# Layer norms of a two-block transformer kernel: gamma and beta applied on token rows by VectorE, layers unrolled

## The reference, cut to what matters

```python
def _layernorm(x, g, b):
    mu = jnp.mean(xf, -1, keepdims=True)
    xc = xf - mu
    var = jnp.mean(xc * xc, -1, keepdims=True)
    y = xc * lax.rsqrt(var + LN_EPS) * g + b

for l in range(DEPTH_2):          # 2 layers
    x = _layernorm(ALPHA * x + 0.5 * _swiglu(x, ffn1_w_in[l], ffn1_w_out[l]), ln1_g[l], ln1_b[l])
    mix = _hybrid_mixer(x, l, ...)        # attention, state space and stick-breaking branches
    x = _layernorm(ALPHA * x + mix, ln2_g[l], ln2_b[l])
    x = _layernorm(ALPHA * x + 0.5 * _swiglu(x, ffn2_w_in[l], ffn2_w_out[l]), ln3_g[l], ln3_b[l])
```

## Time and profile before

| what | us |
|---|---|
| median of three runs | 2288.71 |
| span of the profiled execution | 2284.1 |
| TensorE matmul busy | 2143.6 (94%) |
| VectorE busy | 1436.7 (63%) |
| ScalarE busy | 1127.0 (49%) |
| GpSimd busy | 140.9 (6%) |
| granted TensorE clock, mean | 0.966 |

### The profile page before, as it was taken

How to read it: one execution, slowest core, us unless ns; L and a number is a source line. 1 busy time by engine, 2 the same in 40 slices (tenths; PEclk the granted TensorE clock), 3 DMA queues, 4 the chain that set the end, 5 groups by cost and what they waited for, 6 DMA issues and landing times.

```text
span 2284.1 us, 38164 instructions
## 1 busy us (share of the span) xinstructions
PE 2143.6 (94%) x14507; PEld 1938.2 (85%) x14507; DVE 1436.7 (63%) x2106; ACT 1127.0 (49%) x1783; POOL 140.9 (6%) x157
## 2 busy tenths in 40 slices
PE   6999899999979999999979979997999999997997
PEld 5788799799868899888979959986989988897995
DVE  6766688465566676566665555556667656666555
ACT  4576466344335586355434433344458635543432
POOL 1200000000010003100010010001000310001002
PEclk9999999999989999999989989998999999998998
DMA  6433455544635344333535544563534333353562
GB/s 220 158 119 125 145 184 184 185 151 163 225 135 190 120 143 132 129 111 112 178 118 184 203 148 148 173 219 129 184 124 136 130 130 111 111 185 112 184 206 88
DMA packets 271155, 350.25 MB, mean 153 GB/s; under 512 B 9915, under 2 KB 225693, under 8 KB 271005
## 3 DMA queue, kind: packets, MB, share of 16 engines
q1 hardware_dynamic: 270733, 347.19, 45.3%
q0 software_dynamic: 272, 1.05, 0.1%
HBM read 347.17 MB, written 1.05 MB: 152 GB/s over the span
## 4 chain that ended last, share of the span: by engine, by line
issue 84%; PE 9%; POOL 4%; DVE 2%; ACT 0%; DMA 0%; SPq 0%; POOLq 0%; DVEq 0%; ACTq 0%
PE ps L650 3%; PE ps L652 2%; PE ps L651 2%; POOL act_s L2186 2%; POOL x L2174 1%; POOL x L2176 1%; DVE ring_r L1531 0%; DMA ring<-in_w_in 0%; PE ps L792 0%; PE ps L820 0%; PE ps L805 0%; POOL small L2151 0%; PE ps L757 0%; DVE act_s L1805 0%; DVE xT_r L1531 0%
## 5 line engine op out<-in xcount | busy, mean ns | idle before, releaser
L1531 DVE TENSOR_TENSOR ring_r<-ring,ring_hi 128x1024 fp32r<-128x1024 f32 x642 | 780.3, 1224 | 539.9 <-ACT ring_hi L1108 536.9
L1108 ACT ACTIVATE ring_hi<-ring 128x1024 fp32r<-128x1024 f32 x642 | 674.9, 1058 | 792.4 <-PE ps L652 737.8
L650 PE MATMUL ps<-xT_hi,ring_hi 128*128 128x256 f32 x2912 | 835.2, 287 | 36.9 <-DVE xT_r L1531 20.3
L651 PE MATMUL ps<-xT_r,ring_hi 128*128 128x256 f32 x2912 | 823.2, 283 | 0.0
L652 PE MATMUL ps<-xT_hi,ring_r 128*128 128x256 f32 x2912 | 823.0, 283 | 0.0
L650 PEld LDWEIGHTS ps<-xT_hi,ring_hi 128*128 128x128 f32 x2912 | 555.6, 191 | 52.3 <-issue 29.9
L651 PEld LDWEIGHTS ps<-xT_r,ring_hi 128*128 128x128 f32 x2912 | 555.6, 191 | 0.1
L652 PEld LDWEIGHTS ps<-xT_hi,ring_r 128*128 128x128 f32 x2912 | 555.1, 191 | 0.0
L652 PE MATMUL ps<-ring_hi,tok_r 128*128 128x512 f32 x536 | 212.6, 397 | 0.0
L650 PE MATMUL ps<-ring_hi,xT_hi 128*128 128x512 f32 x432 | 178.5, 413 | 15.3 <-DVE xT_r L1531 11.5
L651 PE MATMUL ps<-ring_r,xT_hi 128*128 128x512 f32 x432 | 174.2, 403 | 0.0
(11 more groups left out here) (280 smaller groups left out, 2616.7 us busy)
## 6 DMA issues: line engine op xcount, KB each, us to landing
ring<-in_w_mix_in SPq DMA_DIRECT2D x92, 1024.0 KB, 4.9
ring<-in_ffn_w_in SPq DMA_DIRECT2D x88, 1024.0 KB, 5.0
ring<-in_ffn_w_out SPq DMA_DIRECT2D x44, 1024.0 KB, 4.9
ring<-in_w_branch SPq DMA_DIRECT2D x24, 1024.0 KB, 5.3
ring<-in_w_in SPq DMA_DIRECT2D x22, 1024.0 KB, 5.0
ring<-in_w_ffn_up SPq DMA_DIRECT2D x22, 1024.0 KB, 5.0
ring<-in_w_ffn_down SPq DMA_DIRECT2D x11, 1024.0 KB, 5.0
ring<-in_w_mix_out SPq DMA_DIRECT2D x8, 1024.0 KB, 5.0
```

What stands on the lines that cost most here:

```text
L650: pe.matmul(out_, stat[0], mov[0], start=first, stop=False)
L651: pe.matmul(out_, stat[0], mov[1], start=False, stop=False)
L1108: act.activation(half_of(ring_hi[:, s % HIGHS, :], s, q), half_of(ring[:, s % SLOTS, :], s, q), ACT.Copy).then_inc(w_hi, 1)
L1531: return dve.tensor_tensor(lo, whole, hi.bitcast(F32), ALU.subtract)
```

## The change

It is one rewrite of all norms, with what follows from it.

- VectorE applies gamma and beta on token rows, in place in `x`: x minus mean times gamma, then times inverse root plus beta, four `scalar_tensor_tensor` of 128x512 a tile. ScalarE's `xhat` and GpSimd's `residual` are gone; GpSimd keeps the roots.
- TensorE transposes `x` itself, each group of four blocks as soon as its half row is normed (`rows_normed`). ScalarE copies all four groups from PSUM into `xT_hi`, and VectorE subtracts them from the same PSUM banks into `xT_r`. The plain `xT` is no longer written.
- The order on VectorE around a norm is by token tile, and each piece of 128x512 is added as soon as its own products are done. The last slot of an FFN's down product is ordered so that each of the four pieces ends by itself.
- `ahead` is 1 for all FFNs, so one slot of the next run is split ahead of every norm; `after_norm` is gone.
- RMS gains arrive as broadcast rows (three more DMAs of 512 KB, those of `ln` gamma and beta as rows are gone) and are multiplied in on VectorE, two pieces of 128x512 a tile; the norm of `mem` is made in place.
- The loop over layers is unrolled, on all engines. The last norm is not transposed. SyncE stores the output in four DMAs of 256 KB, each when its piece is normed.

```diff
-            with dve.Fori(0, LAYERS) as L:
-                def layer_norm(k, slots, s, free=None):
-                    dve.wait_ge(x_ready, x_count(L, 2 * k))
-                    for t in range(T):
-                        add_x(L, slots, 4 + k, s, t, base)
-                        wait_added(L, t, base, free)
-                        for n in range(2):
-                            link(dve.bn_stats(st[:, 6 * n:6 * n + 6], x[:, t, n * BANK:(n + 1) * BANK]))
...
-                        ask_root(L, dve.tensor_scalar(v[:, 2:3], v[:, 1:2], LN_EPS / ALPHA ** 2, None, ALU.add))
-                        dve.scalar_tensor_tensor(v[:, 3:4], v[:, 0:1], -1.0, v[:, 2:3], ALU.mult, ALU.mult).then_inc(stat_ready, 1)
-                    norm_cols(L, 4 + k, cols[:, g:g + 8], cols[:, b:b + 8], xT, xT_hi, xT_lo, 4 if k == 1 else 0)
+            for L in range(LAYERS):
+                def layer_norm(k, wait_part, s, of_bank, banks_free=None):
+                    dve.wait_ge(gb_loaded, 2 * 16 * (3 * L + k + 1))
+                    def part(t, n):
+                        wait_part(t, n)
+                        ins_ = added(t, n, b, s)
...
+                        link(dve.bn_stats(stats[:, t, 6 * n:6 * n + 6], x[:, t, n * BANK:(n + 1) * BANK]))
+                    def spread(t):
...
+                        link(dve.bn_aggr(v[:, 0:2], stats[:, t, :]))
+                        return ask(dve.tensor_scalar(v[:, 2:3], v[:, 1:2], LN_EPS / ALPHA ** 2, None, ALU.add))
+                    def affine(t, root_at):
+                        done = [link(dve.scalar_tensor_tensor(p_, p_, v[:, 0:1], gb[:, 0, g * BANK:(g + 1) * BANK], ALU.subtract, ALU.mult))
+                                for g, p_ in enumerate(parts)]
+                        dve.wait_ge(root_done, root_at)
+                        for g, p_ in enumerate(parts):
+                            sync(done[g])
+                            dve.scalar_tensor_tensor(p_, p_, v[:, 2:3], gb[:, 1, g * BANK:(g + 1) * BANK], ALU.mult, ALU.add).then_inc(rows_normed, 1)
+                    early = ((0, 0), (1, 0), (0, 1)) if banks_free else ((0, 0), (0, 1))
+                    for t, n in early:
+                        part(t, n)
+                    affine(0, spread(0))
+                    for t, n in ((1, 0), (1, 1)):
+                        if (t, n) not in early:
+                            part(t, n)
+                    root_at = spread(1)
+                    if not last:
+                        norm_lows(event, 0, xT_hi, xT_lo, base)
+                    affine(1, root_at)
+                    if not last:
+                        norm_lows(event, 1, xT_hi, xT_lo, base)
+            def norm_lows(event, t, hi, lo, base=4):
+                n = slice(t * P, (t + 1) * P)
+                for g in range(2):
+                    k = slice(4 * g, 4 * g + 4)
+                    dve.wait_ge(xT_act, parts_of(event, t, g))
+                    low(lo[:, k, n], bank(base + 2 * t + g).rearrange("p (k n) -> p k n", n=P), hi[:, k, n]).then_inc(xT_dve, 1)
             def norm(...):                                   # TensorE
                 for t in range(T):
-                    pe.wait_ge(hat_ready, lap(L, 2 * event + t + 1, 6))
                     for g in range(2):
+                        pe.wait_ge(rows_normed, parts_of(event, t, g))
                         for k in range(4):
                             tr = pe.transpose(...)
+            def norm_highs(event, hi, base=4):               # ScalarE
+                for t in range(T):
+                    for g in range(2):
+                        act.wait_ge(hat_turned, parts_of(event, t, g))
+                        act.activation(hi[:, 4 * g:4 * g + 4, t * P:(t + 1) * P], bank(base + 2 * t + g)..., ACT.Copy).then_inc(xT_act, 1)
-        f["ahead"] = 1 if f["index"] == 0 else 0
+        f["ahead"] = 1
-                    pool.wait_ge(gb_loaded, lap(L, 32 * (k + 1), 96))
-                    for t in range(T):
-                        pool.wait_ge(hat_ready, lap(L, 2 * (4 + k) + t + 1, 6))
-                        link(pool.tensor_tensor(x[:, t, :], xhat[:, t, :], gb[:, 0, :], ALU.mult))
-                        sync()
-                        pool.tensor_tensor(x[:, t, :], x[:, t, :], gb[:, 1, :], ALU.add).then_inc(x_ready, 1)
...
-            pool.dma_start(out[0].rearrange("(t p) n -> p t n", p=P), x[:, :, :]).then_inc(out_stored, 16)
+                    sp.wait_ge(rows_normed, parts_of(EVENTS - 1, t, g))
+                    sp.dma_start(out[0, t * P:(t + 1) * P, n], x[:, t, n]).then_inc(out_stored, 16)
```

More of the change, by code:

```diff
@@ L682, in half @@
                 s = c.slots[h]
-                if h == 0 and c.event is not None or h == 1 and c.tail:
+                if c.event is not None or h == 1 and c.tail:
                     if q == 0:
@@ L770, in _ @@
             pe.wait_ge(cols_ready, 1)
-            norm(None, 0, xhat)
+            norm(0, xhat)
             def pair1(p):
@@ L863, in _ @@
                         half(None, c, h, q)
-            norm(None, 2, xhat)
-            ffn(None, ffn0, 3)
-            norm(None, 3, x, 0)
-            with pe.Fori(0, LAYERS) as L:
+            norm(2, xhat)
+            ffn(None, ffn0, 2)
+            norm(3, x, 0)
+            for L in range(LAYERS):
                 def turn_rows():
-                    pe.wait_ge(rows_loaded, lap(L, 11 * 16, 11 * 16))
+                    pe.wait_ge(rows_loaded, lap(L, 5 * 16, 5 * 16))
                     b = ffn1["free0"][3] + FFC // 2
@@ L1076, in _ @@
                             half(L, c, h, q)
-                norm(L, 5, xhat)
-                ffn(L, ffn2, 6)
-                norm(L, 6, xhat, 0)
+                norm(norm_event(L, 1), x)
+                ffn(L, ffn2, norm_event(L, 1))
+                if L < LAST:
+                    norm(norm_event(L, 2), x, 0)
         @block.scalar
@@ L1650, in _ @@
             dve.wait_ge(cols_ready, 1)
-            rms_rows(x, 0)
-            norm_cols(None, 0, conv1[:, N_CONV1:N_CONV1 + 8], None, xT, xT_hi, xT_lo)
+            dve.wait_ge(g1_loaded, 16)
+            rms_rows(x, xhat, mix_g, 0)
+            for t in range(T):
+                norm_lows(0, t, xT_hi, xT_lo)
             gain = gains1.rearrange("p (a d) -> p a d", d=HD)
@@ L1837, in wait_added @@
[L1837 to L1850 removed]
+            pairs_of_out, pairs_of_out2 = ({c.index: c.pair for c in o} for o in (out1, out2))
@@ new lines, in _ @@
+            for t in range(T):
+                for n in range(2):
+                    wait_out(None, out1, t, n)
+                    b = 2 * pairs_of_out[n] + t
+                    added(t, n, b, 1.0).then_inc(drained[b], 1)
+                for b in (t, 2 + t):
+                    dve.wait_ge(drained[b], ffn0["free0"][b])
+                dve.sem_inc(x_added, 1)
+            dve.wait_ge(g1_loaded, 2 * 16)
+            rms_rows(x, xhat, ffn_g, 2)
+            for t in range(T):
+                norm_lows(2, t, xT_hi, xT_lo)
@@ L2194, in _ @@
                     elif step[0] == "dnorm":
-                        root(L, small[:, 184:184 + 2 * DH])
-                residual(1)
-                residual(2)
-                chain.leave()
-            pool.wait_ge(x_ready, x_count(LAYERS, 0))
-            pool.dma_start(out[0].rearrange("(t p) n -> p t n", p=P), x[:, :, :]).then_inc(out_stored, 16)
-            pool.wait_ge(out_stored, 16)
+                        root(small[:, 184:184 + 2 * DH])
+                layer_root()
+                layer_root()
     return nc
```

352 lines of the change are left out of this document (154 added, 198 removed).

## The result

| | before | changed |
|---|---|---|
| median of four runs each, us | 2287.84 | 2232.03 |
| span of the profiled execution, us | 2284.1 | 2232.1 |
| granted TensorE clock, mean | 0.966 | 0.974 |
| GpSimd busy, us | 140.9 | 84.1 |

The ratio is 0.9766 [0.9742, 0.9790]: 2.3% faster. The span fell by 52.0 us (forecast 51.5). In a later comparison the ratio was 0.9772 [0.9752, 0.9793]. By these two ratios the change is worth 52 to 54 us.

A forecast was written before the change was run, and what follows sets the result against it. Bound: serial norm chains, mostly on VectorE, while TensorE waits, stretched by GpSimd's residual. Savings 8.8 + 13.6 + 9.8 + 9.4 + 3.2 + 4.2 + 2.5 = 51.5 us give span 2232.6, time 2237 us, range 2215 to 2256.

The forecast's parts named there:

- First norm, E + 11.0: First layer norm of a layer: next product 11.0 us after E, the last product's end, against 15.4; 4.4 saved, twice.
- Second, E + 11.8: Second layer norm of a layer, ffn2 following: next product 11.8 us after the last one's end, against 18.6; 6.8 saved, twice.
- third, E + 11.7: Third layer norm of layer one, at the loop's turn: next product at E + 11.7 us against 21.5; 9.8 saved.
- The RMS norm: Norm ahead of the first block's FFN: next product at E + 7.2 us against 10.4; 3.2 saved.
- The affine operation, 0.65: One VectorE affine operation of 128x512 with two SBUF tensors takes 0.65 us, bounds 0.35 and 1.3.
- End, E + 10.7: Last product to program end: last piece at E + 7.2, DMA 3.0, 0.5 behind; 10.7 us against 20.1, 9.4 saved.
- Plain transposition, 3.7: Transposition between the blocks: four low parts end 3.7 us behind the last product, against 7.9; 4.2 saved.
- Clock, 2.5: TensorE's restarts at the lower clock behind norms: 2.5 us counted as saved, of 15.7 over seven windows.
- Norms at the head, 0: Norm at the program's head and norm of `mem`: taken as 0, bounds 1.8 us gained and 1.5 lost.
- the stretching stays: Rival: something other than GpSimd's wide operations holds VectorE; 6.3 us in each of five norms return, 2269 us; chance 0.06.
- Instruction streams: Rival: longer unrolled lists make engines pause for new instructions; 38 pauses on TensorE's path, about 2310 us; slower's chance 0.04.
- The clock stays up: Rival: shorter pauses at the norms no longer let TensorE's clock fall; 13 us more saved, 2224 us; chance 0.18.

## Why the prediction was right

Sign and cause came out as forecast, and the time within its range: 2232.03 against 2237.0 us. Some 2.8 of the 5.0 us between them come from the 4.6 that were added to the span, where the runs show 1.7 to 1.9. That the sum of savings came so near, 52.0 against 51.5, is in part luck. The terms of the windows add up to 49.0 and measured 47.9, and in them the end was forecast 0.8 too low, the norms 0.2 too low to 0.9 too high. The 4 us outside the windows, which fill the gap, differ from one execution to the next: the second profile of the changed kernel is 5 us shorter with the same windows. By its steps:

- *First norm, E + 11.0:* 10.86. VectorE began at E - 2.89 (forecast 2.7), its chain took 12.74 us (12.7, each of its parts within 0.2), and the product came 1.01 behind it (1.0). The last term holds by two errors that cancel: tile 1's eight transpositions end 1.36 behind the last affine operation, not 0.98, but the first product's record begins 0.35 before their end.
- *Second, E + 11.8, third, E + 11.7:* 12.23 and 12.24. The chain ended at E + 9.41 (forecast 9.5). The tail was 2.82 instead of 2.3 us. The lower clock was in the forecast (0.98 for the last four transpositions); what it had left out is that the four ahead of them, begun at 1142.59, still run when the last affine operation ends, so that all eight end 1.36 us behind it; the copy (0.60) and the low part (0.69) follow. The RMS norm took 8.16 instead of 7.2: 0.5 of it is the same tail (2.83), and 0.4 is a chain that ended at E + 5.3 instead of 4.9.
- *The affine operation, 0.65:* one by itself takes 0.74 by its record (24 of them: 0.741 to 0.746), the spacing is 0.66. For the chain the spacing counts, so the term held.
- *End, E + 10.7:* 9.91. The last affine operation ended at E + 7.46 (7.2), and from there to the end it took 2.45 us instead of 3.5. The term that was mis-sized is the DMA, 3.0 forecast, and 2.0 by its median row:

```profile
out<-x SPq DMA_DIRECT2D x4, 256.0 KB, 2.0
```

  It lies below the lower bound of 2.7, which a load of 64 KB had given (the same load takes 4.6 in the changed kernel): a smaller transfer of another kind is no bound for a store.
- *Plain transposition, 3.7:* 3.69. *Clock, 2.5:* in part. The window of the plain transposition now stands at 1.00, but in the ten us behind it the clock is 0.83 in the one profile and 1.00 in the other, against 0.75 before; that saves 0.8 or 2.5 us. The forecast had counted on the better case. *Norms at the head, 0:* the product behind the first starts at 24.69 instead of 24.63, and the window of `mem` is 7.70 instead of 7.18.
- *Unrolling and `ahead`:* the first at 2 us at the turn and nothing elsewhere was confirmed. The second was held in the terms of the third norm and of the plain transposition, without a size of its own; it is 4.2 us in those windows.

Of the rivals, *the stretching stays* fell twice: without GpSimd's wide work the old kernel has short operations, and with it the new kernel has long ones. *Instruction streams* fell with the unrolled kernel before. *The clock stays up* did not happen by itself (0.60 to 0.67 in the five windows between products). Idle transpositions held it at 1.00 in three of the five and at 0.88 and 0.85 in the others, and gave 4.6 us, not 13. Much of the time at the lower level lies where TensorE waits anyway: by twice (1 - clock) times the length it is some 50 us in the windows of the changed kernel, out of 116 us in its whole span.

The Trainium skill gives the rule (GPSIMD Engine Reference, Specifications) that VectorE and GpSimd contend where a VectorE instruction has two SBUF inputs or runs in a two-port mode. The runs agree as to the shift, the low parts and the affine operations, which have two SBUF inputs (0.16 to 2.29 us, and 1.40 to 2.97 a pair). The cast has one; whether it runs in a two-port mode no run shows. Beside the roots the victim was not the one that I had weighed. I had looked only at VectorE's side of the earlier trace rows, where nothing was long, and taken 0; it is right for the path, since the root, which does grow to 0.99 us, ends at 646.90, before the second affine pair starts at 647.07. In the last norm, where tile 1's root also stands beside affine operations, it takes 0.98 too, and VectorE again does not wait.

## What to carry to other kernels

Where VectorE is the chain that TensorE waits for, look at what GpSimd does at the same time, before anything is rewritten: here 31 of 48 us in the windows came from GpSimd's wide SBUF work beside VectorE's, 8 more from the same work ahead of the output, and one wait that put it under the products brought over half of the whole gain. Order work on the chain's engine so that the other engines' latencies fall on something useful (1.4 us a norm), and put work that is not needed next behind what is waited for (1.2 us a norm). A waiting TensorE can be kept at its full clock with idle transpositions, worth about 5 us here over five norms by the medians.

## What the runs showed of the hardware that was not expected

- Contention works both ways. A 128x1 root on GpSimd takes 0.55 us beside VectorE operations with a PSUM input and 0.99 beside affine operations with two SBUF tensors, whose own time does not change. When both sides are wide, both grow: 3.3 instead of 2.3 to 2.7 us on GpSimd, 2.3 to 2.7 instead of 1.2 on VectorE.
- What is stretched is not a matter of two SBUF inputs alone: a cast with one SBUF input went from 0.43 to 1.39 us. Nor is it one of size: a 128x1 operation with two such inputs went from 0.16 to 2.29, and ended with the GpSimd operation beside it (661.21 and 661.19). Operations that read PSUM were not stretched where they stood beside GpSimd's wide work (four of 128x128 in 1.35 us either way).
- A store of 256 KB landed 2.0 us behind its issue, faster than loads of 64 KB in the kernel before (2.7 us) and in the changed one (4.6).
